# Conv tails flipped in output order, group squares summed on VectorE, shift sums of nine columns, and second-block scores taken straight from the first block's tokens

## The chip, the cores and the metric

The kernel runs on one core of a Trainium2 chip. The metric is the device time of one execution in microseconds (us), as the median of several runs. The core has TensorE (PE, with its weight loads listed as PEld), VectorE (DVE), ScalarE (ACT), GpSimd (POOL) and SyncE (SP). Everything is float32 except a few bfloat16 selections and sums.

## The reference, cut to what matters

One layer of a hybrid decoder runs for a prompt of 256 tokens and for 8 samples of one token each; all weights are shared. The parts that the change touches:

```
mod = silu(c) @ w_mod + b_mod             # c: one row for the prompt, 8 for the samples = nine columns
sh1, sc1, gt1, sh2, sc2, gt2 = split(mod, 6)
proj = h @ w_in                           # q | k | v | forget | z | xBC | dt | gate A | gate B

# Branch B, Mamba-2
xa = concat([conv0, xbc]);  conv_new = xa[:, -3:]          # the "tails", 3 rows x 3072 columns per stream
u = silu(conv(xa));  xs, bm, cm = split(u, (2048, 512, 512))
# ssd_scan, 2 chunks of 128 tokens, 4 groups of 8 heads:
y_diag = einsum('bctsg,bctsgr,bcsgrp->bctgrp', cb, lmat, xd)
st     = einsum('bcsgn,bcsgr,bcsgrp->cbgrpn', bm, decay_end, xd)
y_off  = einsum('bctgn,bctgr,cbgrpn->bctgrp', cm, exp(acs), s_prev)   # s_prev of chunk 1 is st of chunk 0
y = (y_diag + y_off + d_skip * xs) * silu(z)
y = y * rsqrt(mean(y*y over each of 4 groups of 512) + EPS) * g_ssm

x  = x + gt1 * ((sigmoid(ga) * (oA @ w_pa) + sigmoid(gb) * (y @ w_pb)) @ w_o)
h2 = rms_norm(x) * (1 + sc2) + sh2
logits = h2 @ w_router + b_router         # 16 experts, 2 per token, SwiGLU of width 512
```

## The kernel before, in words

Data lies with channels on the 128 partitions; the 256 prompt tokens and 8 samples are 264 columns. Every engine walks one list, `jobs`, in the same order and does its own part of each job. Semaphores tie the parts together. Seven PSUM banks are dealt to the jobs in turn (`bank_of`): a job waits until the engine that reads the bank's former tenant is done. So the list sets the order on every engine, and leaving jobs out also moves the banks of those behind.

The jobs that matter here, in their order:

- ("mod", 5), ("ct", 0), ("sp"): the last modulation part; the first sixth of the conv tails flipped (four chunks of 128 channels by 27 tail entries become 27 rows of 512) and sent out in two DMAs from ACT's queue; and the probabilities of the samples' attention turned, copied by ACT (L1013, L1014).
- ("so", 0), ("ct", 1), ("sx", 0), ("z", 0) to ("z", 3), ("so", 1), ("ct", 2), ("sx", 1). so is the samples' attention output, four samples at a time, 12 matmuls of 512 columns on the cached values; sx turns it. z is a projection of 128 columns: 8 matmuls of 264 columns. The value pages of samples 4 to 7 go into the buffers that so 0 reads, so POOL loads them (L799, in `in_cache_v`, eight loads) only when so 0 is done, and so 1 waits for them (L1864 and the line above it).
- bs, bt, xs: rows of B, C and x with tokens on the partitions (L1680). ACT copies them and, between bs and bt, issues five DMAs to scratch (L1032 to L1037); the last of them loads the skip weights, which DVE awaits (L1429) before the first block's decays.
- For each block a of 128 tokens: cb (B times C in the block), ab (sums of decays, L1907), y (scores times x, L1921). Between them stand the z jobs 4 to 15, and ct 3, ct 4 and ct 5.
- Ahead of block 1, s1 (L1889) makes the state that block 0 leaves: four matmuls of 512 columns, copied by ACT (L1041). y of block 1 adds a second matmul per head (L1924) on that state and on `ce`, which POOL makes as exp(sums) times C (L824). Before that, POOL decays x (`xe`, L806) for both blocks, scales `xe` of block 0 by the whole decay of block 1 (L813) and issues five small DMAs (L816, L818).
- For y of block 1 DVE also applies the gate z, squares and adds the two chunks of a job (L1456 to L1458). yp (L1999) sums these squares over the partitions: per group two accumulated matmuls of 256 columns.
- fs (L1933) makes the prompt's last state. Then the samples' state updates (ssm, on DVE from L1466 on, ACT L1080, POOL's loads and stores) run beside the gates g and the projection pa (L1993).
- yn, sw, pb, shr: the norm of the samples' y; the products of the second shift with the router weights, 18 matmuls of 16 columns (L1941 to L1946); the projection pb (L2011), which waits for yn's result; and the shift turned into rows: four jobs of four flips. The prompt's row goes out to scratch (L1096) and comes back in another layout (L1103).
- o, lg, hx, rk, then the expert part: pairs of experts with their weights streamed by SP into 22 places (L597).

Of the kernel before, what the change touches and what calls it, by code (L numbers as in the profile page):

```python
# [14 lines left out]
ALU = mybir.AluOpType  # L15
# [3 lines left out]
D = 1024  # L19
# [32 lines left out]
def build(nc, t):  # L52
    ctx = ExitStack()
    with ctx:
# [66 lines left out]
        mrow = early[:, 1281:1537]  # L121
        stT = sb("conv_states", [128, NCB, 24])
# [50 lines left out]
        s1T = part(DI)  # L173
# [4 lines left out]
        ce = part(3 * 512).rearrange("p (s k) -> p s k", s=3)  # L178
        ctok = (cw[:, 2 * XW:2 * XW + 512], cw[:, 0:512])
# [5 lines left out]
        prod_lo = part(NXB * NST // 2)  # L185
        st0 = part(NXB * NST)
        prod_hi, bx = part(NXB * NST // 2), part(NXB * NST)
# [12 lines left out]
        shrow_p = attT[:].rearrange("p c t -> p (c t)")[0:1, D:2 * D]  # L200
# [51 lines left out]
        for c in range(8):  # L252
# [37 lines left out]
        jobs += [("pb", i) for i in range(4)] + [("shr", i) for i in range(4)] + [("pb", i) for i in range(4, 8)]  # L290
# [10 lines left out]
        for n, j in enumerate([j for j in jobs + late if j[0] not in NOBANK]):  # L301
            if j == ("bt", 0):
                turned = 5
# [273 lines left out]
        def _(sp):  # L577
# [125 lines left out]
            sp.wait_ge(o_tail, 16 * 12)  # L703

        @block.gpsimd
        def _(pool):
# [112 lines left out]

            for b in range(8):  # L820
# [38 lines left out]
            pool.wait_ge(o_tail, 16 * 12)  # L859
# [26 lines left out]
        def _(act):  # L886
# [48 lines left out]
            for j in jobs:  # L935
                k = j[0]
                if k == "sm":
# [4 lines left out]
                                             "sk", "sp", "so", "ct", "bs", "bt", "s1", "fs", "z", "g", "yp", "yn",  # L942
# [75 lines left out]
                elif k == "ct":  # L1018
                    i = j[1]
                    if i > 1:  # L1020
                        act.wait_ge(o_tail, 32 * i)
                    release(act, fn(ctok[i % 2][0:27, :], ps[0:27, :], ACT.Copy), j)
                    act.dma_start(t["conv_sample"].rearrange("o b w c -> (o b w) c")[:, 512 * i:512 * i + 512],
                                  ctok[i % 2][0:24, :]).then_inc(o_tail, 16)
                    act.dma_start(t["conv_prompt"].rearrange("o b w c -> (o b w) c")[:, 512 * i:512 * i + 512],
                                  ctok[i % 2][24:27, :]).then_inc(o_tail, 16)
# [13 lines left out]
                elif k == "s1":  # L1040
                    release(act, fn(s1T[:, 512 * j[1]:512 * j[1] + 512], ps[:], ACT.Copy), j)  # L1041
# [1198 lines left out]
```

## Time and profile before

| | |
|---|---|
| median of 3 runs | 774.99 us (773.93 to 775.7) |
| profiled execution, its span | 772.6 us |
| around the span, against the median | 774.99 - 772.6 = 2.4 us |
| PE busy in the span | 731.8 us (95%) |
| DVE, ACT, POOL busy | 377.3, 290.5, 98.6 us |
| HBM over the span | 285 GB/s |

The span is the time from the first to the last instruction of one profiled execution. A busy PE is not a PE that sets the end: a stretch belongs to whatever ends its last wait. A float32 matmul leaves two records in the trace, so "x16" of a 264-column form is 8 matmuls, one z job.

### The profile page before, as it was taken

What the parts mean: (1) busy time and instruction counts of PE and PEld (TensorE: products, weight loads), DVE (VectorE), ACT (ScalarE), POOL (GpSimd) and SP (SyncE); (2) the same over time, 40 slices, a digit from 0 to 9 for tenths busy, and PEclk for the clock granted to TensorE, in tenths of its full rate; (3) what the DMA queues carried; (4) which work ended last, traced back from release to release, by engine and by line L of the source; (5) the groups of instructions that cost most, each with busy time, mean ns of one, the idle gap of its engine ahead of it and who ended that gap; (6) DMA issues with size and microseconds to landing.
All of it is one profiled execution on the core that took longest, in us unless ns stands there. A gap on an engine that the chain in (4) does not pass through costs nothing.

```text
span 772.6 us, 12374 instructions
## 1 busy us (share of the span) xinstructions
PE 731.8 (95%) x4469; PEld 501.9 (65%) x4469; DVE 377.3 (49%) x959; ACT 290.5 (38%) x678; POOL 98.6 (13%) x169
## 2 busy tenths in 40 slices
PE   3899999999999989999999999999999999999986
PEld 3475687778785667888877888887634344434433
DVE  1364337777774087587999311112513244324423
ACT  3221157656774224668885001012522122212201
POOL 4331021122110113430110000000010000000000
PEclk9999999999999999999999999999999999999998
DMA  9996374969775621349999697467999999999991
GB/s 314 331 346 223 119 203 153 341 218 323 256 280 185 207 61 58 117 139 375 370 313 325 231 377 238 148 263 294 339 420 422 416 421 422 417 421 421 417 380 60
DMA packets 88650, 219.48 MB, mean 284 GB/s; under 512 B 11990, under 2 KB 55598, under 8 KB 75145
## 3 DMA queue, kind: packets, MB, share of 16 engines
q1 hardware_dynamic: 73360, 181.71, 64.3%
q0 software_dynamic: 7840, 31.67, 12.0%
q10 hardware_dynamic: 7384, 5.25, 2.2%
q8 instruction: 38, 0.62, 0.3%
q14 instruction: 28, 0.22, 0.1%
HBM read 207.07 MB, written 13.22 MB: 285 GB/s over the span
## 4 chain that ended last, share of the span: by engine, by line
PE 70%; DVE 8%; DMA 8%; ACT 6%; issue 4%; SPq 1%; ACTq 1%; POOLq 1%; POOL 0%; DVEq 0%
PE bank L1770 16%; PE bank L2103 13%; PE bank L2011 8%; PE bank L2128 6%; PE bank L2019 4%; PE bank L1680 3%; PE bank L1763 3%; PE bank L1993 3%; DMA conv_out<-in_w_mod 3%; DMA arena<-in_w_up 3%; PE bank L2155 2%; PE bank L1720 2%; DMA arena<-in_state_ssm 2%; DVE arena L1466 2%; DVE arena L1470 1%
## 5 line engine op out<-in xcount | busy, mean ns | idle before, releaser
L1770 PE MATMUL bank<-h_normed,weight_ring 128*128 128x264 f32 x1024 | 237.4, 388 | 1.7 <-ACT conv_work L1088 1.7
L1770 PEld LDWEIGHTS bank<-h_normed,weight_ring 128*128 128x128 f32 x1024 | 191.2, 190 | 36.9 <-issue 4.2
L2103 PE MATMUL bank<-arena,h_normed 128*64 128x512 f32 x136 | 60.3, 594 | 0.0
L2011 PE MATMUL bank<-y_T,weight_ring 128*128 128x264 f32 x256 | 59.0, 394 | 0.4 <-DVE y_T L1503 0.4
L2011 PEld LDWEIGHTS bank<-y_T,weight_ring 128*128 128x128 f32 x256 | 49.6, 195 | 9.2 <-issue 0.5
L1587 DVE TENSOR_TENSOR arena<-arena,bank 128x512 f32<-128x512 f32 x8 | 8.4, 1053 | 85.4 <-PE bank L2103 85.4
L1680 PE MATMUL bank<-identity,arena 128*128 128x128 f32 (+5 forms) x218 | 30.5, 280 | 13.7 <-ACT arena L904 9.3
L1080 ACT ACTIVATE arena<-conv_out,early_small 128x128 f32<-128x128 f32 x128 | 38.3, 387 | 10.8 <-DVE arena L1466 10.2
L2128 PE MATMUL bank<-arena 128*64 128x512 f32 x88 | 39.2, 595 | 0.0
L873 POOL DMA_INDIRECT h_normed<-h_scratch,token_rows x7 | 7.1, 1020 | 250.3 <-DVE token_rows L1554 135.1
L1390 DVE SCALAR_TENSOR_TENSOR conv_work<-conv_work,conv_out 128x288 f32<-128x288 f32 x72 | 37.6, 522 | 2.5
L1680 PEld LDWEIGHTS bank<-identity,arena 128*128 128x128 f32 (+5 forms) x218 | 26.0, 148 | 17.4 <-issue 11.0
L2103 PE MATMUL bank<-conv_out,h_normed 128*64 128x512 f32 x76 | 34.7, 594 | 2.7 <-DMA arena<-in_w_up 2.6
L1134 ACT ACTIVATE h_normed<-bank,conv_tails 128x128 f32<-128x128 f32 x64 | 17.4, 383 | 51.5 <-PE bank L1680 47.9
L1594 DVE SCALAR_TENSOR_TENSOR x_residual<-bank,conv_out,x_residual 128x256 f32<-128x256 f32 x64 | 30.0, 475 | 9.1 <-PE bank L2151 5.9
L2103 PE MATMUL bank<-weight_ring,h_normed 128*64 128x512 f32 x112 | 31.7, 592 | 0.0
L1993 PE MATMUL bank<-att_T,weight_ring 128*128 128x264 f32 x128 | 28.9, 387 | 1.6 <-ACT arena L1086 1.6
L1763 PE MATMUL bank<-h_normed,weight_ring 128*64 128x264 f32 x256 | 29.8, 388 | 0.0
L1512 DVE TENSOR_TENSOR arena<-arena,bank 128x264 f32<-128x264 f32 x8 | 3.4, 429 | 53.6 <-PE bank L2011 53.6
L2019 PE MATMUL bank<-arena,weight_ring 128*128 128x264 f32 x128 | 29.4, 388 | 0.0
L2103 PEld LDWEIGHTS bank<-arena,h_normed 128*64 128x64 f32 x136 | 18.3, 137 | 16.0 <-issue 16.0
L1993 PEld LDWEIGHTS bank<-att_T,weight_ring 128*128 128x128 f32 x128 | 24.2, 190 | 6.1 <-ACT arena L1086 2.0
(403 smaller groups left out, 1224.2 us busy)
## 6 DMA issues: line engine op xcount, KB each, us to landing
weight_ring<-in_w_in SPq DMA_DIRECT2D x36, 1024.0 KB, 6.4
weight_ring<-in_w_mod SPq DMA_DIRECT2D x22, 1024.0 KB, 9.7
arena<-in_w_down SPq DMA_DIRECT2D x11, 1024.0 KB, 23.7
arena<-in_w_gate SPq DMA_DIRECT2D x10, 1024.0 KB, 13.7
weight_ring<-in_w_down SPq DMA_DIRECT2D x10, 1024.0 KB, 14.6
weight_ring<-in_w_up SPq DMA_DIRECT2D x9, 1024.0 KB, 24.9
arena<-in_state_ssm POOLq DMA_DIRECT2D x8, 1024.0 KB, 12.0
out_ssm_sample<-arena POOLq DMA_DIRECT2D x8, 1024.0 KB, 8.8
```

The lines of the kernel that those rows point to most:

```text
L1080: ins = fn(bx[:, NST * c:NST * c + NST], bc[:, b, 0, :], ACT.Copy, scale=xdt[:, c, b:b + 1])
L1134: ins = fn(xg[:, c, :], banks[5 + h][:, 128 * q:128 * q + 128], ACT.Identity, bias=shq[:, c:c + 1])
L1390: link(v.scalar_tensor_tensor(acc, x[:, w:w + XO], vec[:, 104 + 24 * w + i:105 + 24 * w + i], acc, ALU.mult, ALU.add), conv_ready if w == ...
L1594: v.scalar_tensor_tensor(xT[:, c, 0:NP], comb_bank(c, last)[:, 0:NP], modT[:, 40 + c, NS:NC], xT[:, c, 0:NP], ALU.mult, ALU.add)
L1680: return tr(out, x, ident[0:k, 0:k])
L1763: ins = mm(ps[64 * x:64 * x + 64, 0:T], slot(s)[:, c, o:o + HD], hT[:, c, :], start=c == 0, stop=c == KD - 1, tile_position=(0, 64 * x))
L1770: ins = mm(ps[:, 0:T], w, hT[:, c, :], start=c == 0, stop=c == KD - 1)
L1993: ins = mm(ps[:, 0:T], w, attT[:, c, :], start=c == 0, stop=c == KD - 1)
L2011: ins = mm(ps[:, 0:T], w, yT[:, c, :], start=c == 0, stop=c == NXB - 1)
L2019: ins = mm(ps[:, 0:T], slot(s)[:, c, 128 * (i % 2):128 * (i % 2) + 128], gT[:, c, :], start=c == 0, stop=c == KD - 1)
L2103: ins = mm(banks[i][BLK * e:BLK * e + BLK, :], xg[:, 4 * h + c, BLK * e:BLK * e + BLK], ws[e][c], start=h == 0 and c == 0, stop=h == 1 and ...
L2128: ins = mm(banks[2 + q][BLK * e:BLK * e + BLK, :], aT[:, 2 * h + c, BLK * e:BLK * e + BLK], ws[e][c][:, 512 * q:512 * q + 512], start=h == ...
```

## The change

- **Tails.** The tails are stored as (tail entry, chunk) instead of (chunk, entry), so that a flip gives rows of 128 channels in the order of the output. 24 flips in six jobs become four flips of 128 columns (ct 0) and one each of 64 and 72 (ct 1); ct 2 to ct 5 are gone; twelve DMAs become three, of pieces of 512 bytes.
- **Order.** z 3 now stands behind so 1 instead of ahead of it. The banks from bt on are turned by 6 instead of 5.
- **Second block.** s1 and its four copies are gone. cx takes the products of B of block 0 with C of block 1 (four matmuls of 128 columns, one copy). POOL multiplies exp(sums) by cx instead of C. y of block 1 uses `xe` of block 0 directly, and the scaled copy for fs goes to a new buffer `xes`. A buffer of the samples' states moves for it.
- **Squares.** DVE adds the sums of two y jobs (one more addition of 256 columns per group), and yp is one matmul.
- **Shift sums.** sw takes all nine columns at once: 9 matmuls of 16 columns instead of 18. A new job sb, behind pb 0, spreads the prompt's row over the partitions with one matmul.
- **Shift rows.** The prompt's two shr jobs are gone. Its row goes to scratch straight from `modT`, in 1024 pieces of 4 bytes.

The diff, cut to its core:

```diff
-        s1T = part(DI)
+        xes = part(DI)
+        cbx = work[:, 0:SG * 128].rearrange("p (g k) -> p g k", g=SG)
...
-        jobs += [("so", 0), ("ct", 1), ("sx", 0)] + [("z", i) for i in range(4)] + [("so", 1), ("ct", 2), ("sx", 1)]
+        jobs += [("so", 0), ("ct", 1), ("sx", 0)] + [("z", i) for i in range(3)] + [("so", 1), ("z", 3), ("sx", 1)]
...
-                jobs += [("s1", g) for g in range(4)]
+                jobs += [("cx",)]
...
-        jobs += [("pb", i) for i in range(4)] + [("shr", i) for i in range(4)] + [("pb", i) for i in range(4, 8)]
+        jobs += [("pb", 0), ("sb",)] + [("pb", i) for i in range(1, 4)] + [("shr", i) for i in range(2)] + [("pb", i) for i in range(4, 8)]
...
-            bk, use = bank_of[("s1", 3)]
-            pool.wait_ge(bank_filled[bk], use)
-            x3 = xe[:, 0, :].rearrange("p (h d) -> p h d", d=HD)
-            link(g.tensor_tensor(x3, x3, tokc[:, 192:224].unsqueeze(2).to_broadcast([128, SH, HD]), ALU.mult), xe_ready)
+            link(g.tensor_tensor(xes.rearrange("p (h d) -> p h d", d=HD), xe[:, 0, :].rearrange("p (h d) -> p h d", d=HD), tokc[:, 192:224].unsqueeze(2).to_broadcast([128, SH, HD]), ALU.mult), xe_ready)
...
-                cv3 = u[:, 20 + b // 2, 128:256].unsqueeze(1).to_broadcast([128, 4, 128])
+                cv3 = cbx[:, b // 2, :].unsqueeze(1).to_broadcast([128, 4, 128])
...
-                    i = j[1]
-                    if i > 1:
-                        act.wait_ge(o_tail, 32 * i)
-                    release(act, fn(ctok[i % 2][0:27, :], ps[0:27, :], ACT.Copy), j)
...
+                    if j[1] == 0:
+                        release(act, fn(ctok[0], ps[:], ACT.Copy), j)
+                        act.dma_start(to_s[0:512].rearrange("(r p) c -> p r c", p=128),
+                                      ctok[0].rearrange("p (r c) -> p r c", c=128)).then_inc(o_tail, 16)
...
-                    if j[1] == 3:
-                        act.dma_start(sh_d, shrow_p).then_inc(rows_out, 16)
+                    if f == 1:
+                        read_out(act, ("modt", 3))
+                        act.dma_start(sh_d.rearrange("o (c p) -> p (o c)", p=128), modT[:, 24:32, NS], allow_slow_non_contiguous=True)\
+                           .then_inc(rows_out, 16)
...
-                        v.tensor_tensor(u[:, 2 * b, 0:NP], u[:, 2 * b, 0:NP], u[:, 2 * b + 1, 0:NP], ALU.add)\
-                            .then_inc(yp_sq, 1)
+                        link(v.tensor_tensor(u[:, 2 * b, 0:NP], u[:, 2 * b, 0:NP], u[:, 2 * b + 1, 0:NP], ALU.add))
+                        if b % 2:
+                            v.tensor_tensor(u[:, 2 * b - 2, 0:NP], u[:, 2 * b - 2, 0:NP], u[:, 2 * b, 0:NP], ALU.add)\
+                                .then_inc(yp_sq, 1)
...
-                elif k == "s1":
-                    g = j[1]
-                    read_out(pe, ("bt", 0))
-                    pe.wait_ge(xe_ready, 1)
-                    ins = mm(ps[:], btok[:, 0, 128 * g:128 * g + 128], xe[:, 0, 512 * g:512 * g + 512],
-                             start=True, stop=True)
+                elif k == "cx":
+                    for g in range(SG):
+                        ins = mm(ps[:, 128 * g:128 * g + 128], u[:, NXB + g, 0:128], u[:, NXB + SG + g, 128:256],
+                                 start=True, stop=True)
...
-                            ins = mm(o, s1T[:, 64 * h:64 * h + 64], ce[:, b % 3, 128 * i:128 * i + 128],
+                            ins = mm(o, xe[:, 0, 64 * h:64 * h + 64], ce[:, b % 3, 128 * i:128 * i + 128],
...
+                        mm(ps[0:NC, 0:NE], modT[:, 24 + c, :], wr[:, c, :], start=c == 0, stop=False)
+                    ins = mm(ps[0:NC, 0:NE], onesf[0:1, 0:NC], brow[:], start=False, stop=True)
```

PE's order around the second half of the samples' attention output, in the kernel before. L1864 is so, `identity,conv_tails` is ct, `identity,arena` is sx, L1770 is z:

```order
L1864 MATMUL bank<-arena 32x512 x12
L1680 MATMUL bank<-identity,conv_tails 27x128 x4
L1680 MATMUL bank<-identity,arena 128x128 x4
L1770 MATMUL bank<-h_normed,weight_ring 128x264 x32
L1864 MATMUL bank<-arena 32x512 x12
L1680 MATMUL bank<-identity,conv_tails 27x128 x4
L1680 MATMUL bank<-identity,arena 128x128 x4
```

The same place in the change, where L1873 is so, L1779 is z and L1689 the flips:

```order
L1873 MATMUL bank<-arena 32x512 x12
L1689 MATMUL bank<-identity,conv_tails 64x128
L1689 MATMUL bank<-identity,conv_tails 72x128
L1689 MATMUL bank<-identity,arena 128x128 x4
L1779 MATMUL bank<-h_normed,weight_ring 128x264 x24
L1873 MATMUL bank<-arena 32x512 x12
L1779 MATMUL bank<-h_normed,weight_ring 128x264 x8
L1689 MATMUL bank<-identity,arena 128x128 x4
```

24 instead of 32 z matmuls now stand between the two so jobs; 8 have moved behind the second, and its four flips of the tails are gone.

PE's order ahead of block 1, before (L1889 is s1, L1894 cb, L1907 ab, L1921 and L1924 y):

```order
L1921 MATMUL bank<-arena 64x128 x12
L1680 MATMUL bank<-identity,conv_out 128x128 x16
L1889 MATMUL bank<-arena 128x512 x4
L1894 MATMUL bank<-conv_out 128x128 x4
L1907 MATMUL bank<-cums_in_parts,head_pick 128x128 x8
L1770 MATMUL bank<-h_normed,weight_ring 128x264 x16
```

The same place in the change (L1900 is cx, L1905 cb, L1918 ab, L1932 y):

```order
L1932 MATMUL bank<-arena 64x128 x12
L1689 MATMUL bank<-identity,conv_out 128x128 x16
L1900 MATMUL bank<-conv_out 128x128 x4
L1905 MATMUL bank<-conv_out 128x128 x4
L1918 MATMUL bank<-cums_in_parts,head_pick 128x128 x8
L1779 MATMUL bank<-h_normed,weight_ring 128x264 x16
```

Four matmuls of 512 columns have become four of 128; nothing else moves here.

## Rows read from the trace of the kernel before

**Rows 1.** PE in order of time, 243 to 274 us: start, length, what, [idle before <-releaser].
```profile
243.93 2.92 PE L1864 MATMUL bank<-arena 128*32 128x512 f32 x24 [1.33 <-issue]
...
248.17 14.41 PE L1770 MATMUL bank<-h_normed,weight_ring 128*128 128x264 f32 x64
263.47 2.92 PE L1864 MATMUL bank<-arena 128*32 128x512 f32 x24 [0.90 <-DMA arena<-in_cache_v]
266.32 0.62 PE L1680 MATMUL bank<-identity,conv_tails 128*27 128x128 f32 x4
...
267.71 3.66 PE L1680 MATMUL bank<-identity,conv_out 128*8 128x128 f32 x32
```
**Rows 2.** The chain that ended last, in order of time: the page load's landing.
```profile
259.22 3.91 DMA arena<-in_cache_v
```
**Rows 3.** ACT in order of time, 242 to 274 us (ACTq is its queue issuing DMAs).
```profile
242.51 0.39 ACTq L1025 DMA_DIRECT2D out_conv_prompt<-conv_work  x1
242.94 0.59 ACT L1013 ACTIVATE arena<-bank 128x128 f32<-128x128 f32 x2 [0.83 <-PE bank L1853]
...
268.43 1.21 ACT L1028 ACTIVATE arena<-bank 8x512 f32<-8x512 f32 x2 [0.71 <-PE bank L1680]
...
272.26 1.23 ACT L1039 ACTIVATE arena<-bank 128x512 f32<-128x512 f32 x2 [2.62 <-issue]
```
**Rows 4.** PE in order of time, 299 to 355 us.
```profile
299.13 3.60 PE L1889 MATMUL bank<-arena 128*128 128x512 f32 x8
302.57 1.05 PE L1894 MATMUL bank<-conv_out 128*128 128x128 f32 x8
...
315.24 0.45 PE L1921 MATMUL bank<-arena 128*64 128x128 f32 x4
...
319.98 0.60 PE L1680 MATMUL bank<-identity,conv_tails 128*27 128x128 f32 x4
```
**Rows 5.** POOL in order of time, 301 to 316 us.
```profile
301.58 3.62 POOL L806 TENSOR_TENSOR arena<-arena,early_small 128x2048 f32<-128x2048 f32 x1 [24.85 <-DVE arena L1415]
...
311.89 3.97 POOL L824 TENSOR_TENSOR arena<-arena,conv_out 128x512 f32<-128x512 f32 x3
```
**Rows 6.** DVE in order of time, 274 to 356 us.
```profile
274.74 2.23 DVE L1429 COPY early_small<-arena 64x16 f32<-64x16 f32 x2 [0.99 <-DMA arena<-in_d_skip]
...
351.23 0.42 DVE L1458 TENSOR_TENSOR conv_out<-conv_out 128x256 f32<-128x256 f32 x1
355.06 1.28 DVE L1466 SCALAR_TENSOR_TENSOR arena<-arena,sample_decays 128x1024 f32<-128x1024 f32 x1 [3.40 <-ACT arena L1080]
```
**Rows 7.** PE in order of time, 354 to 480 us.
```profile
354.73 1.03 PE L1999 MATMUL bank<-conv_out,ones 128*128 128x256 f32 x4
...
402.80 10.95 PE L1770 MATMUL bank<-h_normed,weight_ring 128*128 128x264 f32 x48 [1.73 <-ACT conv_work L1088]
...
418.87 25.19 PE L1993 MATMUL bank<-att_T,weight_ring 128*128 128x264 f32 x112 [1.56 <-ACT arena L1086]
...
447.31 30.34 PE L2011 MATMUL bank<-y_T,weight_ring 128*128 128x264 f32 x128 [0.40 <-DVE y_T L1503]
...
478.37 1.04 PE L1680 MATMUL bank<-identity,conv_out 128*1 128x128 f32 x8
479.24 28.65 PE L2011 MATMUL bank<-y_T,weight_ring 128*128 128x264 f32 x128
```
**Rows 8.** Windows: length, busy (x) of PE, PEld, DVE, ACT, POOL; clock, DMA share, GB/s.
```profile
443.90:447.30 3.40, 3.01 (x39) 2.82 (x38) 1.67 (x9) 1.57 (x2) 0.84 (x4) 0.98 0.59 185
447.30:451.30 4.00, 3.99 (x11) 3.18 (x12) 0.71 (x5) 0.00 (x0) 0.00 (x0) 0.59 1.12 373
...
600.00:740.00 140.00, 138.24 (x732) 56.93 (x730) 49.74 (x150) 32.05 (x75) 5.00 (x5) 1.00 1.02 419
```
**Rows 9.** ACT in order of time, 485 to 513 us.
```profile
485.84 0.36 ACTq L1103 DMA_DIRECT2D conv_tails<-sh_scratch  x1
512.08 0.51 ACT L1105 ACTIVATE h_normed<-x_residual,conv_out 128x256 f32<-128x256 f32 x1 [31.17 <-DVE x_residual L1516]
```

More of the change, by code:

```diff
@@ L121, in build @@
         mrow = early[:, 1281:1537]
+        flat_tails = tails[:].rearrange("p c s -> p (c s)")
+        tails_s = flat_tails[:, 0:24 * NCB].rearrange("p (s c) -> p s c", c=NCB)
+        tails_p = flat_tails[:, 24 * NCB:27 * NCB].rearrange("p (w c) -> p w c", c=NCB)
         stT = sb("conv_states", [128, NCB, 24])
@@ L184, in build @@
         st1, st2 = part(NXB * NST), part(NXB * NST)
-        prod_lo = part(NXB * NST // 2)
+        prod_lo, prod_hi, bx = part(NXB * NST // 2), part(NXB * NST // 2), part(NXB * NST)
         st0 = part(NXB * NST)
-        prod_hi, bx = part(NXB * NST // 2), part(NXB * NST)
         y2 = part(NXB * NS).rearrange("p (l b) -> p l b", b=NS)
@@ L1018, in _ @@
                 elif k == "ct":
-                    i = j[1]
-                    if i > 1:
-                        act.wait_ge(o_tail, 32 * i)
-                    release(act, fn(ctok[i % 2][0:27, :], ps[0:27, :], ACT.Copy), j)
[L1023 to L1026, printed above, removed]
+                    to_s = t["conv_sample"].rearrange("o b w (c p) -> (o b w c) p", p=128)
+                    to_p = t["conv_prompt"].rearrange("o b w (c p) -> (o b w c) p", p=128)
+                    if j[1] == 0:
+                        release(act, fn(ctok[0], ps[:], ACT.Copy), j)
+                        act.dma_start(to_s[0:512].rearrange("(r p) c -> p r c", p=128),
+                                      ctok[0].rearrange("p (r c) -> p r c", c=128)).then_inc(o_tail, 16)
+                    else:
+                        fn(ctok[1][0:64, 0:128], ps[0:64, 0:128], ACT.Copy)
+                        release(act, fn(ctok[1][0:72, 128:256], ps[0:72, 128:256], ACT.Copy), j)
+                        act.dma_start(to_s[512:576], ctok[1][0:64, 0:128]).then_inc(o_tail, 16)
+                        act.dma_start(to_p, ctok[1][0:72, 128:256]).then_inc(o_tail, 16)
                 elif k == "bs":
@@ L1039, in _ @@
                     release(act, fn(btok[:, j[1], :], ps[:], ACT.Copy), j)
-                elif k == "s1":
-                    release(act, fn(s1T[:, 512 * j[1]:512 * j[1] + 512], ps[:], ACT.Copy), j)
+                elif k == "cx":
+                    release(act, fn(cbx, ps.rearrange("p (g k) -> p g k", g=SG), ACT.Copy), j)
                 elif k == "ab":
@@ L1528, in _ @@
                     link(gain(32, 56), gsc_ready)
+                elif k == "sb":
+                    ps = filled(dve, j)
+                    release(dve, v.tensor_copy(shw[:, 0, :], ps[:, 0:NE]), j)
                 elif k == "lgt":
@@ L1871, in _ @@
                     pe.wait_ge(conv_ready, NCB)
-                    for q in range(4):
-                        ins = flip(ps[0:27, 128 * q:128 * q + 128], tails[:, 4 * j[1] + q, :])
+                    if j[1] == 0:
+                        for q in range(4):
+                            ins = flip(ps[:, 128 * q:128 * q + 128], flat_tails[:, 128 * q:128 * q + 128])
+                    else:
+                        flip(ps[0:64, 0:128], flat_tails[:, 512:576])
+                        ins = flip(ps[0:72, 128:256], flat_tails[:, 576:648])
                 elif k == "bs":
@@ L1940, in _ @@
                     for c in range(KD):
-                        mm(ps[:, 0:NE], modT[:, 24 + c, NS:NC].to_broadcast([128, 128]), wr[:, c, :],
-                           start=c == 0, stop=False)
-                    mm(ps[:, 0:NE], onesf[0:1, :], brow[:], start=False, stop=True)
-                    for c in range(KD):
-                        mm(ps[0:NS, NE:2 * NE], modT[:, 24 + c, 0:NS], wr[:, c, :], start=c == 0, stop=False)
-                    ins = mm(ps[0:NS, NE:2 * NE], onesf[0:1, 0:NS], brow[:], start=False, stop=True)
+                        mm(ps[0:NC, 0:NE], modT[:, 24 + c, :], wr[:, c, :], start=c == 0, stop=False)
+                    ins = mm(ps[0:NC, 0:NE], onesf[0:1, 0:NC], brow[:], start=False, stop=True)
+                elif k == "sb":
+                    read_out(pe, ("sw",))
+                    ins = mm(ps[:, 0:NE], ident[0:NC, NS:NC].to_broadcast([NC, 128]), shw[0:NC, 1, :], start=True, stop=True)
                 elif k == "shr":
@@ L1949, in _ @@
                     for q in range(4):
-                        c = 4 * (j[1] % 2) + q
-                        if j[1] < 2:
-                            ins = flip(ps[0:NS, 128 * q:128 * q + 128], shdiff[:, c, :])
-                        else:
-                            ins = flip(ps[0:1, 128 * q:128 * q + 128], modT[:, 24 + c, NS:NC])
+                        ins = flip(ps[0:NS, 128 * q:128 * q + 128], shdiff[:, 4 * j[1] + q, :])
                 elif k == "lg":
@@ L1995, in _ @@
                 elif k == "yp":
-                    for q in range(2):
-                        b = 2 * j[1] + q
-                        pe.wait_ge(yp_sq, b + 1)
-                        ins = mm(ps[:, 0:NP], onesf[:], u[:, 2 * b, 0:NP], start=q == 0, stop=q == 1)
+                    pe.wait_ge(yp_sq, j[1] + 1)
+                    ins = mm(ps[:, 0:NP], onesf[:], u[:, 4 * j[1], 0:NP], start=True, stop=True)
                 elif k == "yn":
```

27 lines of the change are left out of this document (13 added, 14 removed), and 6 rows, old and new, of the table fill.

## The prediction
> **What bounds the kernel now.** I read the engine table first: PE is busy for 95% of the span, so PE is where to look, but the edits sit in places with different limits. So I read next, for each edit, PE in order of time with the releaser in brackets, then ACT, POOL and DVE over the same stretch, and last the windows with the clock and the DMA share. The reader is to see five stretches.
>
> - 243 to 274 us. PE does so 0 at 243.93 behind 1.33 us of waiting, four z jobs, and so 1 at 263.47 after 0.90 us of waiting for a page of cached values [rows 1]. The last page was issued at 259.22 and took 3.91 us, so it landed at 263.13 [rows 2]. Then come the flips bs, bt, xs from 267.71, while ACT copies bs at 268.43, issues DMAs and copies bt at 272.26 [rows 3]. DVE starts on the skip weights at 274.74, as their DMA lands [rows 6], and the first block's products follow that.
> - 299 to 344 us. PE runs without a gap; POOL's first products ce start at 311.89, three in 3.97 us [rows 5], and y of block 1 at 315.24 [rows 4].
> - 355 to 444 us. DVE and ACT update the samples' states. PE waits 1.73 us and 1.56 us for ACT in it [rows 7].
> - 444 to 518 us. pb 0 starts at 447.31 when DVE has normed the samples' y (0.40 us of waiting) [rows 7]. Behind it PE is full.
> - From 600 to 740 us the DMA engines are full (share 1.02, 419 GB/s) [rows 8]. The last expert load therefore lands a fixed time after the stream gets going. What gets it going is PE's progress through pb, o and hx, so a shift before 550 us is carried to the end whole, and nothing that is gained beside the stream is.
>
> **The change part by part**, against the profiled execution's span of 772.6 us; 2.4 us more lie between it and the median.
>
> Tails, ct 0. Still four flips, now of 128 columns instead of 27; a flip's length hardly depends on that, so 0. ACT issues one DMA instead of two ahead of the copies that so 0 waits for (242.94): one issue of 0.39 us and its gap are gone [rows 3]. -0.4 us (0 if the one issue of more pieces takes as long as two). so 0, the page loads behind it on POOL and their landing all move with it: so 1 may start at 263.1.
>
> z 3 behind so 1. One z is 14.41 / 4 = 3.60 us [rows 1]. z 0 starts at about 247.5 (248.17, less 0.4 and two flips), three of them end at 258.3, and the page is not there before 262.75. PE then has nothing for some 4.7 us, where it waited 0.90. After so 1 (start 263.1, followed at 265.9 by z 3 as ct 2 followed it at 266.32) z 3 ends at 269.5 and sx at 269.95, so bs starts at 269.95 instead of 267.71: +2.2 us. That is 3.60 for z 3, less ct 2 (0.5), less sx's wait for ACT (0.3), which z 3 now covers, less the 0.4 from above and rounding. Behind PE stands ACT: bs can be copied at 270.6 instead of 268.43, then the same DMA issues and the bt copies, and DVE gets the skip weights 2.2 us later. Bounds: +1.8 (if ACT makes up the two issues of ct 2) and +3.2 (nothing hidden). I take +2.2, as both PE's and ACT's rows give it.
>
> The clock. Before, in 443.90 to 447.30 PE has only narrow matmuls and a short wait, and the 4.0 us behind that ran at a granted clock of 0.59 on average, that is, part of it at 1.2 instead of 2.4 GHz [rows 8]. It cost the four pb jobs there 30.34 us against 28.65 us for the next four: 1.7 us [rows 7]. A wait of 4.7 us without any matmul is emptier than that stretch, so I take the same fall behind it, on so 1: +1.7. Lower bound 0 (the gap of 1.33 us and its like show no loss), upper bound below as a rival.
> The Trainium skill says the same in "TensorE: Matmul & The Clock Gate", section "What's actually happening": the slow clock is the default and activity releases it. By that rule the 4.7 us cost a fall, and the sum would be the forecast's; without it the sum is the first rival's.
>
> s1 to cx. s1 is 3.60 us, cx is shaped like cb, 1.05 us [rows 4]: -2.55 on PE. ct 3 ahead of it is another -0.5. PE would be ready for y of block 1 at 312.2 on the old time scale. But y waits for the first ce, 311.89 + 3.97 / 3 = 313.2 [rows 5]; POOL starts that series when DVE has read xs (301.58, after 24.85 us of waiting), does the same two large products and the five DMAs as before, and s1 was not what it waited for. So y starts at 313.2 instead of 315.24: -2.0 (bounds 0 and -3.05). ct 4 and ct 5 come later where PE is full, a good 0.45 us each (0.60 long with the tail of the pipeline [rows 4]): -0.9. ACT loses copies, so exponentials are not late.
> fs therefore starts at +2.2 - 2.0 - 0.9 = -0.7 without the clock's part.
>
> Squares. DVE: four additions of 0.42 us. Two lie under DVE's waits, two end just ahead of the states, where DVE then waits 3.40 us for ACT [rows 6]: 0, and 0.8 if that cover went. PE: four matmuls of half of 1.03 us [rows 7], -2.0 on PE. But PE stands in the 1.73 and 1.56 us waits behind ACT, and ACT behind DVE's chain of states; the waits grow. 0 (bound -2.0).
>
> Shift sums. Nine matmuls less between yn and pb 0, but pb 0 is released by DVE at 447.31 [rows 7]. 0, and no more to gain than the time PE has in hand. sb adds one small matmul behind pb 0, 0.15.
>
> Shift rows. Eight flips less where PE is full: 479.24 - 478.37 = 0.87 us [rows 7]. With sb: -0.7. The stored row was fetched again at 485.84 and ACT's next work is at 512.08 [rows 9], so the store has some 26 us to spare.
>
> Sum: -0.7 + 1.7 - 0.7 = +0.3 us. 772.6 + 0.3 + 2.4 = 775.3 us.
>
> **The rivals.**
>
> The clock holds. For it: PE waits 1 to 2 us in several places before and stays at full clock. Against it: the one sparse stretch of 3.4 us lost it. Then the sum is -1.4: 773.6 us.
>
> The gates are soft: POOL's ce does not hold y (1.05 more) and yp's 2.0 us come through, with the clock held: -1.4 - 3.05 = -4.4, 770.5 us. For it: matmuls dominate the chain. Against: the brackets name ACT and POOL.
>
> Slower: the clock stays low until so 1 and z 3 are done. These are 2.92 + 3.60 = 6.5 us of work, which double: +6.5 instead of +1.7, a sum of +5.1, 780.1 us. The price passes no change once over 3 us of work run at half clock. For it: so 1 itself starts from rest, as pb 0 did. Against: pb lost only 1.7.
>
> Slower too: s1's time is not given back. y of block 1 is gated by POOL with 1 us to spare, and if the products come 2 us later against DVE than before (new buffers, DVE busier beside them), -2.0 becomes 0: +2.3, 777.3 us. Against it: POOL's instructions have the same count and shape.
>
> The scattered row is late. 1024 pieces of 4 bytes go beside pb's weight loads; from a store of over 30 us on, ACT's first o job is late and the router behind it, 777 us with 2 us too much. Against: the old row was back for its next step well ahead.
> The Trainium skill ("DMA: Bandwidth & Descriptors", section "Specifications") has transfers under 512 bytes done as read-modify-write, and its rules give one descriptor to each element of a strided last dimension; by that this rival's store is slow, but no row shows by how much.
>
> **How the numbers follow.** Clock falls, as summed: 0.43, 775.3 us, its own range 773.8 to 776.8 for the bounds of z 3 and of ce. Clock holds: 0.28. Soft gates: 0.08. Low clock through z 3: 0.07. s1 not returned: 0.10. Late row: 0.04. 0.2% (1.55 us, about what a measurement tells from no change) reaches from 773.44 to 776.54. Faster: the soft gates, half of "clock holds", a little of the first: 0.27. Slower: the three slow rivals and a small part of the first: 0.21. The same: 0.52. The range leaves out the soft gates and the low clock through z 3 and takes in the rest: 772.0 to 778.0.
>
> **What would show it.** Ahead of the second so PE waits 4 to 5 us for `in_cache_v`, and the windows behind show a clock under 1.0: the forecast; at 1.0: the first rival. DVE's copy of the skip weights stands 2 us later than 274.74 (4 with the fall). y's first matmul of block 1 names POOL as its releaser, with about 1 us. fs starts 0.7 us earlier than before, or 1.0 later with the fall. PE's waits among g and pa grow by about what yp saves. pb 0 is still released by DVE. The prediction is wrong if the second so waits under 2 us, if y of block 1 starts without a wait, or if the expert stream's length changes by over 1 us.

## The result: 0.46% slower, and the profile after

The changed kernel takes 779.24 us (median of 20 runs, 773.64 to 783.09) against 774.84 us for the kernel before (20 runs on the same chip). The ratio is 1.0046, with an interval of 1.0032 to 1.0060. The forecast was 775.3 us and its range ended at 778.0. The profiled execution has a span of 777.1 us at a mean granted clock of 0.986, against 772.6 us at 0.995.

PE in the stretch of [rows 1 and 4], after (start, duration, engine, line, what is written and read, count, idle time before and its releaser):

```profile
244.81 2.92 PE L1873 MATMUL bank<-arena 128*32 128x512 f32 x24 [0.95 <-issue]
249.05 10.85 PE L1779 MATMUL bank<-h_normed,weight_ring 128*128 128x264 f32 x48
264.48 4.49 PE L1873 MATMUL bank<-arena 128*32 128x512 f32 x24 [4.58 <-DMA arena<-in_cache_v]
268.90 3.83 PE L1779 MATMUL bank<-h_normed,weight_ring 128*128 128x264 f32 x16
273.00 3.74 PE L1689 MATMUL bank<-identity,conv_out 128*8 128x128 f32 x32
318.72 0.45 PE L1932 MATMUL bank<-arena 128*64 128x128 f32 x4 [1.02 <-POOL arena L824]
346.50 7.41 PE L1944 MATMUL bank<-arena 128*128 128x128 f32 x64
```

So 1 waits 4.58 us for its page and then runs 4.49 us instead of 2.92. y of block 1 waits 1.02 us for POOL. The four fs jobs (346.50) start 2.6 us later than before. Not all of that is the change's: ahead of every edit, one group of matmuls (L1729, which was L1720) took 5.32 us in this execution and 3.66 us in that of before, and the next such group stands 1.2 us late (238.41 instead of 237.22). So fs is 1.4 us late on the scale of this execution. Before, then after:

```profile
18.07 3.66 PE L1720 MATMUL bank<-weight_ring,early_small 128*32 128x256 f32 x64
237.22 3.66 PE L1720 MATMUL bank<-weight_ring,early_small 128*32 128x256 f32 x64
343.92 7.41 PE L1933 MATMUL bank<-arena 128*128 128x128 f32 x64
```

```profile
18.53 5.32 PE L1729 MATMUL bank<-weight_ring,early_small 128*32 128x256 f32 x64
238.41 3.66 PE L1729 MATMUL bank<-weight_ring,early_small 128*32 128x256 f32 x64
```

PE in the stretch of [rows 7], after:

```profile
405.44 13.71 PE L1779 MATMUL bank<-h_normed,weight_ring 128*128 128x264 f32 x48 [3.24 <-ACT conv_work L1091]
418.98 28.64 PE L2000 MATMUL bank<-att_T,weight_ring 128*128 128x264 f32 x128
447.46 0.30 PE L2007 MATMUL bank<-small,ones 128*128 128x32 f32 x2
450.89 9.04 PE L2016 MATMUL bank<-y_T,weight_ring 128*128 128x264 f32 x32 [2.50 <-DVE y_T L1510]
481.65 1.04 PE L1689 MATMUL bank<-identity,conv_tails 128*8 128x128 f32 x8
```

The wait ahead of the last three gate jobs has grown from 1.73 to 3.24 us, and the jobs from 10.95 to 13.71 us. The wait ahead of pb 0 has grown from 0.40 to 2.50 us. The windows (stretch, length, busy PE, PEld, DVE, ACT, POOL, granted clock, DMA share, GB/s) say why jobs are long:

```profile
264.00:268.00 4.00, 3.52 (x20) 0.78 (x24) 0.00 (x0) 0.00 (x0) 0.00 (x0) 0.57 0.00 0
404.00:412.00 8.00, 6.56 (x17) 5.20 (x18) 7.93 (x8) 7.93 (x21) 1.06 (x2) 0.57 1.03 335
452.00:456.00 4.00, 4.00 (x13) 3.10 (x12) 0.00 (x0) 0.00 (x0) 0.00 (x0) 0.57 1.12 377
550.00:556.00 6.00, 5.89 (x42) 5.70 (x42) 3.88 (x17) 2.84 (x4) 0.00 (x0) 0.72 0.94 324
600.00:740.00 140.00, 139.85 (x749) 58.60 (x749) 54.07 (x171) 32.59 (x78) 4.98 (x5) 1.00 1.02 420
```

and of the kernel before:

```profile
446.00:452.00 6.00, 5.60 (x34) 4.53 (x35) 1.90 (x11) 0.00 (x0) 0.00 (x0) 0.72 1.10 371
764.00:772.00 8.00, 1.24 (x12) 0.79 (x10) 2.06 (x3) 1.18 (x2) 0.00 (x0) 0.75 0.41 144
```

The reader is to see that the losses come in equal portions. Length times (1 - clock) is 4 x 0.43 = 1.7 us behind so 1, 8 x 0.43 = 3.4 us in the gates (two portions), 1.7 us in pb and 6 x 0.28 = 1.7 us at the router's gather. I call 1.7 us of this a fall of the clock, from 2.4 to 1.2 GHz. The profiled execution of the change has five; that of before has one, in pb. Both lose some 2.2 us more within the span in the last microseconds, where PE is nearly idle. I take that as free.

The same reading of the windows places every fall of the 14 profiled executions (the kernels are those of the experiments below):

| place (start of the fall) | profiles with a fall there |
|---|---|
| so 1 (263 to 265 us) | the change, z_only, yp_two |
| just ahead of y of block 0 (278 to 283) | z_only, yp_two, so_warm, zb_yp2, pb_warm, best, sq_fill |
| gates (395 to 409) | two each in the change, pb_warm, yp_two; one each in so_warm, sq_fill, sq_late, sq_only, zb_yp2 |
| pb (446 to 457) | before, cx_only, the change, so_warm, sq_fill, sq_late, yp_two, zb_yp2 |
| router's gather (550 to 556) | the change, pb_warm, sq_fill, yp_two |
| none | z_back, zb_fill |

Only the fall on so 1 keeps to one edit: it is in all three profiles where PE waits empty for the page there (3.8 to 4.6 us), and in no other. The slow group at 18 us is in five profiles (the change, pb_warm, so_warm, sq_fill, yp_two: 5.3 to 5.5 us); these have three to six falls, the nine others none to three, and all four falls at the gather are theirs. The windows show a clock of 1.00 at that group, so it isn't counted as a fall. What ties it to the falls isn't shown, but one profile is no fair sample of a kernel's falls.

All executions can be counted, since each comes with its span and mean clock: falls = ((1 - clock) x span - 2.2) / 1.7, to the nearest whole number. The commonest execution of before (0.995) has 1, the profiled one of the change 5. Within the 16 sets of executions (6 to 33 each; two executions with a mean clock of 0.66 and 0.85 are left out) one fall more goes with 1.39 us more of span. The table gives for each kernel the mean span, the mean number of falls, and the span less 1.39 us for each fall, in short the span without falls. It is an estimate from a fit: single executions lie 1.1 us around it, so a mean of 6 is good to 0.5 us and one of 20 to 0.25. The ratio is the measured one to the kernel before.

| kernel | ratio (interval) | mean span | falls | without falls |
|---|---|---|---|---|
| before (three sets) | 1 | 773.4 to 774.1 | 1.1 to 1.4 | 771.8 to 772.1 |
| the change | 1.0046 (1.0032, 1.0060) | 777.0 | 5.2 | 769.8 |
| z_only | 1.0080 (1.0055, 1.0106) | 779.2 | 3.7 | 774.1 |
| z_back | 0.9971 (0.9952, 0.9990) | 771.0 | 2.4 | 767.7 |
| so_warm | 0.9996 (0.9983, 1.0009) | 772.9 | 2.5 | 769.4 |
| sq_only | 1.0024 (1.0005, 1.0043) | 775.2 | 1.8 | 772.8 |
| sq_fill | 1.0030 (1.0004, 1.0056) | 775.6 | 1.8 | 773.0 |
| yp_two | 1.0069 (1.0046, 1.0091) | 778.9 | 4.9 | 772.1 |
| zb_yp2 | 1.0006 (0.9982, 1.0029) | 773.7 | 2.8 | 769.9 |
| pb_warm | 1.0005 (0.9986, 1.0023) | 774.3 | 2.2 | 771.3 |
| sq_late | 1.0004 (0.9980, 1.0027) | 774.3 | 2.3 | 771.1 |
| cx_only | 0.9989 (0.9969, 1.0008) | 773.1 | 1.7 | 770.7 |
| zb_fill | 0.9940 (0.9916, 0.9964) | 769.1 | 0.7 | 768.2 |
| best | 0.9937 (0.9915, 0.9960) | 769.2 | 1.2 | 767.5 |

So the change takes 2.2 us out of the work and adds 4.0 falls, 5.6 us. That is 3.4 us, beside 2.9 to 3.6 us between the mean spans and 4.4 us between the medians of all runs. The split hangs on the 1.39 us: with the 1.57 us that the fall on so 1 cost its own row, it would be 2.9 and 6.3 us.

### The profile page after: what moved, and what is told of

Its sections match the earlier page's. It is cut to its first block, busy times and chain, and to the rows that moved or that the text cites. A ratio compares the mean times of both kernels' runs of the same rounds, so it can differ in the third digit from the quotient of the medians.

```text
span 777.1 us, 12251 instructions
## 1 busy us (share of the span) xinstructions
PE 731.0 (94%) x4419; PEld 500.1 (64%) x4419; DVE 382.3 (49%) x963; ACT 285.0 (37%) x670; POOL 98.8 (13%) x169
## 4 chain that ended last, share of the span: by engine, by line
PE 60%; SPq 11%; DVE 9%; ACT 6%; DMA 6%; issue 4%; POOL 2%; ACTq 1%; POOLq 1%; DVEq 0%
PE bank L1779 17%; SPq L599 8%; PE bank L2016 8%; PE bank L2108 6%; PE bank L2024 4%; PE bank L2000 4%; PE bank L2133 4%; SPq L597 3%; PE bank L1772 3%; PE bank L1689 3%; PE bank L1729 3%; DMA arena<-in_w_up 3%; DMA arena<-in_x_sample 1%; DVE arena L1473 1%; ACT arena L1083 1%
## 5 line engine op out<-in xcount | busy, mean ns | idle before, releaser
L1779 PE MATMUL bank<-h_normed,weight_ring 128*128 128x264 f32 x1024 | 240.7, 391 | 3.3 <-ACT conv_work L1091 3.2
L1779 PEld LDWEIGHTS bank<-h_normed,weight_ring 128*128 128x128 f32 x1024 | 193.0, 192 | 40.4 <-issue 5.1
L2016 PEld LDWEIGHTS bank<-y_T,weight_ring 128*128 128x128 f32 x256 | 49.5, 194 | 11.3 <-issue 2.6
L1689 PE MATMUL bank<-identity,arena 128*128 128x128 f32 (+5 forms) x218 | 31.0, 283 | 13.6 <-ACT arena L904 9.3
L1689 PEld LDWEIGHTS bank<-identity,arena 128*128 128x128 f32 (+5 forms) x218 | 26.5, 151 | 17.1 <-issue 10.7
L2024 PEld LDWEIGHTS bank<-arena,weight_ring 128*128 128x128 f32 x128 | 24.1, 190 | 5.2 <-issue 1.3
```

What stands on the lines that cost most here:

```text
L1689: return tr(out, x, ident[0:k, 0:k])
L1779: ins = mm(ps[:, 0:T], w, hT[:, c, :], start=c == 0, stop=c == KD - 1)
L2016: ins = mm(ps[:, 0:T], w, yT[:, c, :], start=c == 0, stop=c == NXB - 1)
L2024: ins = mm(ps[:, 0:T], slot(s)[:, c, 128 * (i % 2):128 * (i % 2) + 128], gT[:, c, :], start=c == 0, stop=c == KD - 1)
```

## The experiments

**z 3 put back, and z 3 alone.**

```
z_back (on the change):  [so 0, ct 1, sx 0, z 0 to 3, so 1, sx 1]
z_only (on before):      [so 0, ct 1, sx 0, z 0 to 2, so 1, z 3, ct 2, sx 1]
```

> The change with z 3 put back ahead of so 1. Theory 1 (the page wait ahead of so 1 and the fall of the clock behind it are the main cost): so 1 waits about 1 us instead of 4.58, the clock stays at full speed there, bs starts some 3.5 to 4 us earlier than in the change, and the time is 3 to 4 us under the change's: 0.999 to 1.000 of the kernel before, or a little under. Theory 2 (the falls of the clock at the gates and at the router are the main cost): this gains under 2 us on the change, so 1.002 or more of before.

> The kernel before with one edit: z 3 behind so 1. Theory 1: so 1 waits 4 to 5 us, the clock falls, y of block 0 starts 3.5 to 4.5 us later, and all of it reaches the end: 1.004 to 1.006 of before. Theory 2: the later stretches absorb it, under 1.002.

z_back: 773.35 us, 5.9 us under the change. z_only: 781.23 us, 6.5 us over before. z_back's PE, its windows, and then the same for z_only:

```profile
263.22 2.92 PE L1873 MATMUL bank<-arena 128*32 128x512 f32 x24 [0.78 <-DMA arena<-in_cache_v]
399.95 10.95 PE L1779 MATMUL bank<-h_normed,weight_ring 128*128 128x264 f32 x48 [3.24 <-ACT conv_work L1091]
```

```profile
262.00:268.00 6.00, 4.36 (x35) 1.59 (x35) 0.25 (x2) 1.05 (x3) 0.00 (x0) 1.00 0.58 191
400.00:412.00 12.00, 12.00 (x54) 10.28 (x55) 11.89 (x14) 8.14 (x24) 1.07 (x2) 1.00 1.03 349
444.00:456.00 12.00, 11.53 (x52) 9.66 (x53) 2.08 (x11) 0.00 (x0) 0.00 (x0) 1.00 1.05 401
```

```profile
263.67 4.24 PE L1864 MATMUL bank<-arena 128*32 128x512 f32 x24 [3.83 <-DMA arena<-in_cache_v]
272.38 3.66 PE L1680 MATMUL bank<-identity,conv_out 128*8 128x128 f32 x32
278.79 0.61 PE L1907 MATMUL bank<-cums_in_parts,head_pick 96*128 96x128 bf16 x8 [1.86 <-ACT arena L1039]
279.23 5.47 PE L1770 MATMUL bank<-h_normed,weight_ring 128*128 128x264 f32 x16
```

```profile
262.00:268.00 6.00, 4.33 (x25) 1.00 (x26) 0.00 (x0) 0.00 (x0) 0.00 (x0) 0.72 0.14 51
280.00:284.00 4.00, 4.00 (x12) 3.08 (x11) 3.81 (x11) 0.63 (x1) 1.39 (x1) 0.57 0.00 0
446.00:460.00 14.00, 13.60 (x87) 11.89 (x86) 3.58 (x17) 1.57 (x2) 0.83 (x4) 1.00 0.72 257
```

z's place makes the wait, and the wait is followed by a fall; a second fall sits at 280, behind the next wait, which is 1.86 us here and was 1.32 us, without a fall, in the kernel before. In pb, where before fell, this execution did not. Without falls the new place costs 2.1 us (769.8 - 767.7) and 2.1 us (774.1 - 772.0), which is the forecast's 2.2. The falls cost 2.8 x 1.39 = 3.9 us and 2.5 x 1.39 = 3.5 us more. Theory 1 of both had the direction and was too small: it priced one fall, and the averages have 2.5 and 2.8. Only the one on so 1 is located; four profiles without z's new place also have a fall ahead of y of block 0, so that z's place brings the one at 280 isn't shown.

**The wait ahead of so 1 filled.**

```
+ if second half: 10 matmuls of 264 columns into the scratch bank   # ahead of so 1
```

> The change with ten matmuls of 264 columns without use (some 4 us) between z 2 and so 1, inside the wait for the page. They take the empty stretch away and leave the wait. If the fall of the clock is worth what the trace shows (so 1 takes 4.49 us instead of 2.92), this is 1.5 us under the change and so 1 is back at 2.92 us; theory 1 then splits into 2.2 us for the wait and 1.6 us for the clock. If the clock doesn't matter to the end: the same as the change.

It came out at 774.26 us, 5.0 us under the change, where one fall would have been 1.5. Its PE shows:

```profile
260.25 4.61 PE L1868 MATMUL bank<-x_residual 128*128 128x264 f32 x20
265.03 2.92 PE L1876 MATMUL bank<-arena 128*32 128x512 f32 x24 [0.17 <-DMA arena<-in_cache_v]
```

The order, the page and its landing are those of the change; only PE isn't empty. so 1 runs at full speed, the time without falls stays (769.4 against 769.8), and the falls drop from 5.2 to 2.5. This separates the wait from its clock: of the 6.0 us between the mean spans of the change and z_back, the useless matmuls take back 4.1, and about 2 remain for the order. They prevent 2.7 falls per execution, though only one sits on so 1 in the change's profile; how an empty wait here brings falls further on isn't shown.

**The squares alone, and VectorE against TensorE.**

```
sq_only (on before):  VectorE adds the two sums of a group; one matmul of 256 columns instead of two
sq_fill:              the same, with that one matmul done twice
```

> The kernel before with one edit: the squares (one more addition on VectorE, one yp matmul less per group). Theory 1: 0. Theory 2: PE's wait behind ACT among the gates grows from 1.73 to over 3 us, the clock falls there in most runs, and the three gate jobs behind take 13.7 us instead of 10.95: 1 us slower, 1.001 of before. If yp's 2 us were worth something, it would be 0.998.

> The kernel before with the squares' edit (VectorE's extra addition, one sum in place of two), and that one matmul done twice, so that PE is as full as before and VectorE as full as in the change. sq_only, the same without the doubled matmul, came out at ratio 1.0024. Theory 1 (the squares cost through PE's emptier wait and the clock behind it): ratio 0.999 to 1.001, the wait ahead of the gates under 2.2 us or without a fall. Theory 2 (they cost through VectorE's four additions of 0.42 us, on the chain that the gates wait for): ratio 1.002 or more, and the states start about 0.8 us later.

Ratios 1.0024 and 1.0030. Both theories of sq_only miss: 0 lies just outside its interval, and PE's wait ahead of the last three gate jobs is 1.80 us, not over 3. A doubled matmul doesn't bring the loss back, so the loss is not PE's emptiness in yp (theory 1 of sq_fill fails). Theory 2 of sq_fill has the ratio right, and the states start 1.1 us later behind fs than before, but not for its reason: VectorE's 4 x 0.42 us have cover (behind the last of them it waits 5.08 us for ACT in sq_only and 3.00 us in sq_fill). ACT behind the fs jobs shows what it is (ACTq: ACT issues a DMA). sq_only, then the change:

```profile
351.89 0.60 ACT L1053 ACTIVATE arena<-bank 128x512 f32<-128x512 f32 x1 [1.19 <-PE bank L1935]
352.51 3.57 ACTq L1054 DMA_DIRECT2D out_ssm_prompt<-arena  x1
356.21 0.98 ACT L1080 ACTIVATE arena<-conv_out,early_small 128x128 f32<-128x128 f32 x3 [3.73 <-issue]
```

```profile
353.95 0.60 ACT L1056 ACTIVATE arena<-bank 128x512 f32<-128x512 f32 x1 [1.19 <-PE bank L1944]
354.57 0.40 ACTq L1057 DMA_DIRECT2D out_ssm_prompt<-arena  x1
355.15 4.78 ACT L1083 ACTIVATE arena<-conv_out,early_small 128x128 f32<-128x128 f32 x16 [0.61 <-DMA conv_out<-bc_scratch]
```

The fourth store of the prompt states holds ACT for 3.57 us at its issue, and the samples' states, which the gates wait for, start late. In the profiles of before, the change, z_back, so_warm, cx_only and zb_fill it takes 0.39 to 0.40 us, in z_only 0.62; in those of sq_only, sq_fill, zb_yp2, pb_warm and yp_two 3.57, 1.50, 2.21, 2.74 and 2.88 us.

**The squares undone within the change.**

```
yp_two (on the change), zb_yp2 (on z_back):  two matmuls of 256 columns again, no third addition
```

> The change with only the squares' part undone: PE adds the two squares of a group again in two matmuls of 1.03 us together, DVE has four additions less. Theory 1 (the added waiting at the gates is the squares' doing: the wait ahead of z's successors grew from 1.73 to 3.24 us and the clock fell behind it): PE's wait ahead of the gate group is under 2.2 us again, the clock stays at 1.00 behind it, yn starts about 1 us earlier than the change's 447.46, and the time is 0.8 to 2.0 us under the change's. Theory 2 (it is the earlier start of the sample products, z's new place or the shift rows that lengthen the wait): the wait stays at 3.2 us with the fall, and the time equals the change's within 0.5 us. The second so keeps its wait of about 4.6 us in both.

> The change with z 3 put back ahead of the second so and the squares' part undone; cx, the shift sums, the shift rows and the tails stay. Theory 1 (z 3's place costs about 5.8 us, as z_back showed, and the squares 0.8 to 2.0 us more, the two add): ratio to the kernel before 0.993 to 0.997, 769.5 to 772.3 us, below z_back. Theory 2 (the squares cost only where the wait lets the clock fall, and in z_back's trace it did not fall): equal to z_back within 0.5 us, ratio about 0.997. In both PE's wait ahead of the gates shrinks from z_back's 3.24 to about 2 us.

Both are slower than their base: 779.73 against 779.24 us, and 774.59 against 773.35 us; without falls by 2.3 and 2.2 us. Neither theory had that, and both fail. The wait ahead of the gates stays at 3.23 us, beside an ACT that the held issue makes late. So the squares' edit loses 0.8 us on the kernel before and gains 2.2 us in the change, and in the profiles each goes with whether the fourth store's issue is held.

**The fourth store issued behind ACT's first 16 products.**

```
  fs:      if i < 3: store(i)
+ ssm 0:   16 products; store(3)
```

> The kernel before with only the squares' edit (as sq_only, ratio 1.0024), and the last of ACT's four stores of the prompt states issued after ACT's first 16 products for the samples instead of ahead of them. In sq_only's trace that one issue held ACT for 3.57 us, in the kernel before 0.39 us. Theory 1 (the squares cost nothing themselves; they shift the releases so that this store's issue is held up on ACT, and the states and gates behind it are late): ratio 0.997 to 1.001, ACT's first products start within 8.2 us of the fs group (11.8 in sq_only, 8.6 before), and the issue, wherever it is held, delays no product of the first token. Theory 2 (the squares' additions on VectorE cost it): ratio 1.002 or more and the states no earlier.

Ratio 1.0004 (sq_only 1.0024). Its ACT:

```profile
351.14 0.60 ACT L1053 ACTIVATE arena<-bank 128x512 f32<-128x512 f32 x1 [1.19 <-PE bank L1938]
351.87 1.57 ACT L1081 ACTIVATE arena<-conv_out,early_small 128x128 f32<-128x128 f32 x5
353.17 0.39 ACTq L1085 DMA_DIRECT2D out_ssm_prompt<-arena  x1
```

ACT's first product starts 8.2 us behind fs, as theory 1 had it, and without falls the kernel is 1.7 us under sq_only. The measured intervals of the two overlap, so theory 1 rests on the estimate and the row. Why one kernel's issue is held and another's isn't, I didn't settle: the squares' edit shifts when VectorE frees the ring for SyncE's two loads of 1 MB each, which land in the queues beside POOL's state loads at the same time, but the rows show only the coincidence.

**cx alone.**

```
- 4 x s1 (1 matmul of 512 columns each)   + cx (4 matmuls of 128 columns), xes and cbx, POOL's order
```

> The kernel before with only the second token block's scoring changed: cx in place of the four s1 jobs, the xes and cbx buffers and POOL's order with it. Theory 1 (the forecast's: POOL's first product gates y of block 1, so 2.0 of s1's 2.55 us come back; the pb fall stays): fs starts 2.0 us earlier, y of block 1 waits about 1 us for POOL, ratio 0.9969 to 0.9980. Theory 2 (a wait grows later and gives it back): fs 2.0 us earlier but pb's first job less than 1 us earlier, ratio 0.999 to 1.000.

773.95 us, ratio 0.9989, 1.3 us less without falls. Neither theory holds: both had fs 2.0 us earlier, and it is 1.0 us earlier (343.31 instead of 343.92, in an execution 0.4 us late at the L1720 group). This build also rotates the banks otherwise, and it has new waits ahead of y of block 0; that the banks cause them isn't shown:

```profile
244.25 2.92 PE L1862 MATMUL bank<-arena 128*32 128x512 f32 x24 [1.28 <-issue]
269.78 2.84 PE L1678 MATMUL bank<-identity,conv_out 128*128 128x128 f32 x24 [0.74 <-DVE att_T L1405]
281.36 0.66 PE L1917 MATMUL bank<-arena 128*64 128x128 f32 x8 [2.82 <-issue]
314.66 0.45 PE L1917 MATMUL bank<-arena 128*64 128x128 f32 x4 [0.64 <-POOL arena L822]
```

From so 0 to y of block 0 it needs 37.1 us, 0.9 more than before; from there to y of block 1 33.3 us, against 35.1. So s1's part gives 1.8 us there, with POOL as the new releaser, as the forecast had it.

**The other two waits filled.**

```
pb_warm (on zb_yp2):  9 useless matmuls ahead of pb 0
zb_fill (on z_back):  6 ahead of gate job 13, 5 ahead of pb 0
best:                 zb_fill, with the fourth store issued late
```

> As zb_yp2, and nine useless matmuls of 264 columns (their sums are overwritten) between the switch matmuls sw and pb's first job, where PE waits 2.50 us for DVE's normed y. Theory 1 (an empty wait lets the clock fall in some executions and 9 filler matmuls prevent it): time 0.3 to 1.5 us under zb_yp2's, the first four pb jobs at full clock (29 us for four). Theory 2 (the clock behind that wait does not depend on what is in it): equal to zb_yp2 within 0.3 us; or up to 0.3 us longer if the filler runs over y's landing.

> z_back (z 3 back ahead of the second so, everything else as in the change), and useless matmuls in two waits of PE: six of 264 columns ahead of gate job 13, where PE waits 3.24 us, and five ahead of pb's first job, where it waits 2.50 us. In pb_warm nine took 4.27 us, so these are 2.8 and 2.4 us and end before the data. Theory 1 (both waits let the clock fall in most executions, though not in z_back's profiled one; z_back's mean clock over its executions was 0.991 to 0.993 at the median): median clock 0.996 or more, no row of the gates or of pb stretched, time 2 to 4 us under z_back's median of 773.35, ratio 0.992 to 0.995. Theory 2 (the waits do not matter to the clock): clock and time as z_back, ratio about 0.997, or a little over for filler that overruns.

> zb_fill with the last store of the prompt states issued behind ACT's first 16 products, as in sq_late. Theory 1 (the held issue happens in some executions of this kernel too): up to 1 us under zb_fill, ratio 0.990 to 0.995. Theory 2 (with the squares' edit and the other edits together the issue is never held): equal to zb_fill within 0.3 us. If the later store holds ACT ahead of the gates' sigmoids instead, a little slower than zb_fill.

pb_warm has zb_yp2's ratio (1.0005 and 1.0006), so its theory 2 holds: its filler takes 4.27 us where 2.50 were free, so 1.4 us come back as work for 0.6 falls less. zb_fill has fitting sizes:

```profile
396.18 2.83 PE L1710 MATMUL bank<-x_residual 128*128 128x264 f32 x12
399.57 10.95 PE L1782 MATMUL bank<-h_normed,weight_ring 128*128 128x264 f32 x48 [0.56 <-ACT conv_work L1091]
441.59 2.49 PE L2018 MATMUL bank<-x_residual 128*128 128x264 f32 x10
444.07 7.39 PE L2021 MATMUL bank<-y_T,weight_ring 128*128 128x264 f32 x32
```

```profile
396.00:412.00 16.00, 15.44 (x70) 12.88 (x69) 15.80 (x17) 12.02 (x33) 1.07 (x3) 1.00 1.03 343
440.00:456.00 16.00, 16.00 (x88) 13.15 (x87) 3.33 (x14) 1.57 (x2) 0.83 (x4) 1.00 0.91 339
```

The falls drop from 2.4 to 0.7, the ratio from 0.9971 to 0.9940 (the ends of the intervals touch) and the median from 773.35 to 770.97 us: theory 1 holds, but for a median clock of 0.995 instead of 0.996. z_back's own profiled execution had no fall at either wait, with 3.24 and 2.50 us of nothing; the filler's worth shows only over many executions. best, 770.62 us, is zb_fill within what can be told apart, as its theory 2 said. Both beat both kernels: the change's edits, but for z 3's place, take 0.3% off alone (z_back) and 0.6% with the two waits filled. No run filled a wait of the kernel before, so how much of the 0.6% filler alone would give there is open.

## Why the prediction was wrong, step by step

- **z 3 behind so 1, +2.2: right.** The wait is 4.58 us (4.7 forecast), the step without falls 2.1 us in both experiments. Behind it ACT copies bs at 273.70 instead of 268.43, that is 4.1 us late on the scale of this execution, and y of block 0 comes 4.2 us late, where +2.2 and the fall made 3.9. VectorE's copy of the skip weights is later than forecast, 5.1 us instead of 4, because one of ACT's issues ahead of it took 1.84 us instead of 0.94.
- **The clock, +1.7: the step that failed.** The fall on so 1 was right in kind and size: the profiled so 1 lost 1.57 us. But the forecast counted one fall more, and the change has four more on average. z's place brings 2.5 to 2.8 falls in the averages, of which the profiles locate one, on so 1; the lengthened waits at the gates and pb bring the rest as far as z_back shows (1.2). The forecast's bound above (a low clock through z 3, 780.1 us) had nearly the right time and the wrong mechanism: the clock is back within so 1 (0.57 in 264 to 268) and falls again elsewhere. The Trainium skill has it in "TensorE: Matmul & The Clock Gate", section "What's actually happening", that activity releases the fast clock. The runs agree: filler brought the falls from 5.2 to 2.5 and from 2.4 to 0.7. But an empty wait didn't always cost a fall: behind 3.24 us z_back's profile has none.
- **s1 to cx, -2.0, and the late tails, -0.9: right.** In the change y of block 0 to y of block 1 is 33.2 us against 35.1, POOL releases it with 1.02 us of waiting, and from there to fs another 0.9 us are saved.
- **Squares and shift sums, 0: right in work, wrong in what I left out.** From fs to yn z_back needs 100.07 us and before 99.97. PE's waits grew from 3.29 to 4.80 us in z_back, about what yp saves, as forecast. But I priced longer waits at nothing. Ahead of the gates (3.24 us) and of pb 0 (2.50 us) they carry falls: two and one in the change's trace (the one in pb was there before, too), and 1.2 more per execution in z_back than in before, 1.7 us. That these waits carry them is what zb_fill shows, whose filler leaves 0.7. A wait that grows was not free.
- **Shift rows and sb, -0.7: half of it.** From pb 0 to the second group of pb jobs it is 31.6 us against 31.9, each with one fall: eight flips less give 0.9 us, and sb, with the break that it makes, takes 0.5 instead of 0.15. ACT fetches the scattered row at 495.47, 11.3 us after the issue, and needs ACT again at 515.35, so the late-row rival falls.
- **Tails, -0.4: nearly right.** so 0's wait is 0.95 us instead of 1.33. From the L1729 group at 238.41 to so 0 the change needs 6.40 us; so do the seven other profiles with the tails' edit (6.40 to 6.41), where those with the old tails need 6.63 to 6.71: 0.3 us.

Together: -1.4 without the clock was forecast, -2.2 measured; 1.7 for the clock was forecast, 5.6 measured. The chances followed the same error: the slower side had 0.21, all of it in rivals about a low clock at one place, POOL's products and the scattered row, none for falls spread over the kernel. It was also added up too small. The three slow rivals make 0.21 by themselves and leave nothing for the part of the first that was to be in it. And the bounds named for the forecast's own range, +3.2 for z 3 and 0 for ce, give 778.3 at its upper end, not 776.8.

What stays open: which of the waits falls in which execution. The same 3.24 us ahead of the gates cost two falls in the change's trace and none in z_back's, and pb 0's 0.40 us fell in before and not in z_only. Open too is why the fourth store is held.

## What to carry to other kernels

Where PE is the bound, price a wait twice: its length, and a chance of a fall of the clock (1.4 us of span here) behind it and further on. The chance grew here even where an edit only emptied PE beside another engine's chain. Read the mean clock of every execution, not the profiled one alone: before you argue about an edit, split each difference into falls and the rest. And where a transfer can't come sooner, matmuls of no use, sized a little under the wait, can be worth more than they cost.

## What the runs showed of the hardware

- Losses by the clock came in portions of 1.7 us (length times one minus the granted clock), one or two at a place, in the 12 of 14 profiles that have any ahead of the last microseconds.
- The issue of one 256 KB store held ACT for 0.39 us in some kernels and for 1.5 to 3.6 us in others, and all of ACT's work behind it.
- A useless float32 matmul of 264 columns costs 0.46 us of PE (ten: 20 records, 4.61 us), so overrunning a wait by three costs as much as a fall.
- Flips of chunks 27 and 128 columns wide take nearly the same time, four in 0.62 and in 0.66 us. The width is that of the loaded weights; 128 columns stream through PE in both (`128*27 128x128`, `128*128 128x128`).
